# Two more places for weight chunks, an earlier (1,0) vector, and the first down weights asked for by GpSimd

## The reference, cut to what matters

```python
cs = silu(c)
for i in range(2):
    mod = cs @ w_mod[i] + b_mod[i]                    # 1024 x 6144: 24 MB a layer
    sh_m, sc_m, g_m, sh_f, sc_f, g_f = split(mod, 6)
    h = modulate(rmsnorm(x, norm_mix[i]), sh_m, sc_m)
    y = hybrid_ab(h, ...) if i == 0 else multiscale_pool(h, w_pool, pool_scale)
    x = x + g_m * y
    h = modulate(rmsnorm(x, norm_ffn[i]), sh_f, sc_f)
    x = x + g_f * hier_moe(h, ...)
return rmsnorm(x, norm_out)

# hybrid_ab: proj = h @ w_in (q, kv, index queries qi, index key, u, v); attention over
#   the 64 keys that the index scores pick; spatial gating of u by v; concat @ w_o
# multiscale_pool: means over trailing windows of 2, 4, 8, 16 tokens, minus h, per-group
#   256x256 matmul (w_pool), times pool_scale
# hier_moe: 4 groups x 8 experts, softmax over groups, best group, best 2 experts in it;
#   out = sum over experts of (silu(t @ w_gate) * (t @ w_up) * gate) @ w_down
```

## Time and profile before

| what | value |
|---|---|
| time, median of 3 | 732.12 us (731.3 to 732.17) |
| the profiled execution | 731.96 us |
| its span | 729.5 us |
| TensorE busy | 641.2 us (88%) |
| VectorE busy | 372.6 us (51%) |
| ScalarE busy | 174.0 us (24%) |
| read from memory | 268.16 MB, mean 370 GB/s with writes |

### The profile page before, as it was taken

One profiled execution on the slowest core, in us unless ns is written; L12 is line 12 of the kernel. 1 busy time (PEld: TensorE's weight loads), 2 busy tenths in 40 slices (PEclk: granted clock), 3 DMA queues, 4 the chain that ended last, 5 costly groups with the idle time before them and its releaser, 6 DMA issues.

```text
span 729.5 us, 11410 instructions
## 1 busy us (share of the span) xinstructions
PE 641.2 (88%) x4226; PEld 386.8 (53%) x4226; DVE 372.6 (51%) x902; ACT 174.0 (24%) x370; POOL 24.9 (3%) x54
## 2 busy tenths in 40 slices
PE   2699998999998889988899888999898899888994
PEld 1487565466654545445554445775445455455542
DVE  1268868967644533443334477664344334433345
ACT  2113441033411211122112240342113111221113
POOL 5100400000000000000000000000000000000000
PEclk9999999999999999999999999799999999999998
DMA  8999535997699999999999999887999999999991
GB/s 335 351 398 398 174 116 192 410 360 281 256 421 421 421 421 423 422 421 423 422 422 422 417 399 409 338 339 306 423 422 420 420 422 422 422 421 423 422 392 58
DMA packets 49677, 269.61 MB, mean 370 GB/s; under 512 B 3796, under 2 KB 5908, under 8 KB 25072
## 3 DMA queue, kind: packets, MB, share of 16 engines
q1 hardware_dynamic: 48864, 268.22, 90.6%
q0 software_dynamic: 784, 1.00, 0.7%
HBM read 268.16 MB, written 1.05 MB: 369 GB/s over the span
## 4 chain that ended last, share of the span: by engine, by line
PE 48%; DMA 38%; SPq 5%; DVE 5%; issue 2%; ACT 1%; POOL 0%; DVEq 0%; POOLq 0%; ACTq 0%
DMA ring<-in_w_up 35%; PE bank L875 9%; PE bank L854 8%; PE bank L889 5%; PE bank L592 4%; PE bank L739 4%; DMA early_w<-in_w_in 3%; PE bank L804 2%; PE bank L522 2%; PE bank L664 2%; PE bank L674 2%; PE bank L759 1%; PE bank L842 1%; SPq L346 1%; PE bank L627 1%
## 5 line engine op out<-in xcount | busy, mean ns | idle before, releaser
L854 PE MATMUL bank<-ring,arena 128*64 128x256 f32 x1024 | 117.3, 382 | 28.9 <-DMA ring<-in_w_up 28.8
L842 PE MATMUL bank<-ring,arena 128*64 128x256 f32 x1024 | 117.6, 382 | 12.8 <-DMA ring<-in_w_gate 12.8
L1139 ACT CAST xn_parts<-arena 128x512 fp32r<-128x512 f32 x64 | 39.6, 619 | 305.6 <-DVE arena L1591 305.6
L854 PEld LDWEIGHTS bank<-ring,arena 128*64 128x64 f32 x1024 | 71.1, 137 | 74.3 <-DMA ring<-in_w_up 41.2
L875 PE MATMUL bank<-dn_w,hT 128*64 128x512 f32 x480 | 109.5, 598 | 0.7 <-DMA dn_w<-in_w_down 0.7
L842 PEld LDWEIGHTS bank<-ring,arena 128*64 128x64 f32 x1024 | 81.1, 137 | 41.9 <-issue 16.8
L1566 DVE SCALAR_TENSOR_TENSOR hT<-hT,bank 128x256 f32<-128x256 f32 x32 | 19.8, 619 | 118.1 <-PE bank L854 118.1
L889 PE MATMUL bank<-xn_parts,sel 128*128 128x512 f32 x256 | 67.1, 406 | 0.0
L875 PEld LDWEIGHTS bank<-dn_w,hT 128*64 128x64 f32 x480 | 32.0, 136 | 62.4 <-issue 61.0
L1591 DVE SCALAR_TENSOR_TENSOR arena<-bank,hT,gates 128x512 f32<-128x512 f32 x64 | 48.0, 749 | 23.5 <-PE bank L875 23.5
L889 PEld LDWEIGHTS bank<-xn_parts,sel 128*128 128x128 f32 x256 | 45.8, 188 | 20.9 <-issue 12.4
(11 more groups left out here) (282 smaller groups left out, 676.1 us busy)
## 6 DMA issues: line engine op xcount, KB each, us to landing
ring<-in_w_gate SPq DMA_DIRECT2D x32, 2048.0 KB, 13.7
ring<-in_w_up SPq DMA_DIRECT2D x32, 2048.0 KB, 18.2
dn_w<-in_w_down SPq DMA_DIRECT2D x30, 2048.0 KB, 10.3
ring<-in_w_mod SPq DMA_DIRECT2D x23, 2048.0 KB, 16.5
ring<-in_w_in SPq DMA_DIRECT2D x2, 2048.0 KB, 21.1
ring<-in_w_down SPq DMA_DIRECT2D x2, 2048.0 KB, 14.6
early_w<-in_w_in SPq DMA_DIRECT2D x1, 2048.0 KB, 21.0
dn_w<-in_w_in SPq DMA_DIRECT2D x1, 2048.0 KB, 17.2
```

The costliest lines, as they stand in the source:

```text
L842: ins = pe.matmul(bank[2][h * WIN:(h + 1) * WIN, 0:FE], xw[:, b, h, k, :], w[:, h, 0, k, :], start=(k == 0), stop=(k == KT - 1))
L854: ins = pe.matmul(bank[3][h * WIN:(h + 1) * WIN, 0:FE], xw[:, b, h, k, :], w[:, h, 1, k, :], start=(k == 0), stop=(k == KT - 1))
L1139: act.copy(xn_parts[:, 0, b, at], y_s[:, b, at]).then_inc(e["y_hi"], 1)
```

## The change

Line numbers in the diff's words are those of the kernel before; the rows of the changed program below have its own.

- **Places.** Two halves of `arena` (free once the attention's values are done) become places for n1a and n1b, the halves of (1,1). The halves of (1,0) move ahead: n0a is loaded right after m2b, n0b after v. q, v, u and the halves of (0,4) and (0,3) come one or two places later, or in other slots. The expert pairs of layer 0 use slots (1,2) and (0,3) instead of (0,2) and (1,3).
- **(1,0) on PE.** Its first half stands between the third and the fourth group of index scores, its second half after the first two transposes of the attention weights. Both leave the routing stage.
- **Waits of SP.** The first expert pair waits for DVE's use of m3b, the second for m5a and the second output chunk; before they waited for PE's use of n0b and n1b.
- **First down weights of layer 0.** GpSimd (POOL) asks for them after DVE's use of m5b; before, SP did so ahead of its loop.
- **Constant rows.** The row of `norm_mix` is spread ahead of kv and no longer after the scores. `pool_scale` is spread in the middle stage ahead of the pooling matmuls, and DVE reads it from PSUM. The halves of `norm_out` are spread after the first pooling matmul group and after (1,4).
- Smaller: (0,2) is reduced into banks 2 and 7; two semaphores of the experts' loop become one.

```diff
-        front = [..., (("in", "kv"), ATT), (("in", "qi"), EARLY_W),
-                 (m2a, 0), (m2b, 1), (("in", "q"), ATT), (("in", "v"), 3), (("in", "u"), 2), (m4a, 0), (m4b, 1),
-                 (("out", 0), EARLY_W), (("out", 1), 3), (m3a, 0), (m3b, 2), (m5b, ATT), (m5a, 1), (n0a, 0), (n0b, 2), (n1a, 1), (n1b, 3)]
+                 (m2a, 0), (m2b, 1), (n0a, 2), (("in", "q"), ATT), (("in", "v"), 3), (n0b, 0), (("in", "u"), 1),
+                 (("out", 0), EARLY_W), (m4a, 2), (("out", 1), 3), (m4b, 0), (m3a, 1), (m3b, 2), (m5b, ATT), (n1a, ARENA_A),
+                 (m5a, 0), (n1b, ARENA_B)]
-        PAIRS = (((0, 2), (1, 3)), ((0, 1), (2, 3)))
+        PAIRS = (((1, 2), (0, 3)), ((0, 1), (2, 3)))
...
             for n in range(FIRST):                                          # SP
                 slot_freed(sp, n)
-                if plan[n] == m5b:
+                if slot_of(n) in (ARENA_A, ARENA_B) or plan[n] == m5b:
                     sp.wait_ge(S["p_turned"], 6)
                     sp.wait_ge(S["bT_ready"], 1)
+                    sp.wait_ge(S["pv_done"], 4)
                 chunk(n)
...
-                sp.wait_ge(S["chunk_done"], chunk_no[n0b if l == 0 else ("mod", 21)] + 1)
+                if l == 0:
+                    sp.wait_ge(S["dve_used"], by_dve.index(m3b) + 1)
+                else:
+                    sp.wait_ge(S["chunk_done"], chunk_no["mod", 21] + 1)
                 gate_load(l, 0, 0)
                 up_load(l, 0, 0)
-                sp.wait_ge(S["chunk_done"], chunk_no[n1b if l == 0 else ("mod", 23)] + 1)
+                if l == 0:
+                    sp.wait_ge(S["dve_used"], by_dve.index(m5a) + 1)
+                    sp.wait_ge(S["chunk_done"], chunk_no["out", 1] + 1)
+                else:
+                    sp.wait_ge(S["chunk_done"], chunk_no["mod", 23] + 1)
                 gate_load(l, 1, 2)
                 up_load(l, 1, 2)
-                if l == 0:
-                    sp.wait_ge(S["dve_used"], by_dve.index(m5b) + 1)
-                else:
+                if l == 1:
                     sp.wait_ge(S["mix_done"], 10)
-                down(l, 0)
+                    down(l, 0)
...
             power(1)                                                        # POOL
+            pool.wait_ge(S["dve_used"], by_dve.index(m5b) + 1)
+            pool.dma_start(dn_w[:, :].rearrange("p o t d -> p o (t d)"),
+                           w_down[0][0:2].rearrange("o (p t) d -> p o (t d)", t=FT)).then_inc(S["dn_first"], 16)
...
-            head_units(range(6), qiT, kiT, (3, 4, 6), S["score_done"], S["score_relu"])   # PE
+            units = qiT, kiT, (3, 4, 6), S["score_done"], S["score_relu"]
+            head_units(range(3), *units)
+            vector((1, 0), (0,))
+            head_units(range(3, 6), *units)
...
+            pe.wait_ge(S["wsT_copied"], 1)
             reduce((0, 2))
             pe.wait_ge(S["kvnT_ready"], 1)
-            pe.wait_ge(S["wsT_copied"], 1)
...
             turn_p(0)
             turn_p(1)
+            vector((1, 0), (1,))
...
                 if l == 0:                                                  # route
-                    turn_raw(l, (0,)), vector((1, 0), (0,)), turn_raw(l, (1,)), vector((1, 0), (1,))
+                    turn_raw(l)
                 else:
-                    vector((1, 3), (1,)), vector((1, 4), (0,)), turn_raw(l), vector((1, 4), (1,))
+                    vector((1, 3), (1,))
+                    pe.wait_ge(S["row_kept"], 1)
+                    vector((1, 4), (0,)), turn_raw(l), vector((1, 4), (1,))
+                    pe.wait_ge(S["col_kept"], columns.index((1, 3)) - 1)
+                    norm_out_row(1, bank[0])
...
                 if l == 0:
                     vector((1, 1), (0,))
-                    for row, b in ((SCALE_ROW, 2), (OUT_ROW, 4)):
-                        for half in range(2):
-                            pe.matmul(bank[b + half][:, :], ident[:, row:row + 1].to_broadcast([P, P]), rows[:, half * HALF:(half + 1) * HALF],
-                                      start=True, stop=True).then_inc(S["row_done"], 1)
...
+            def norm_out_row(half, to):
+                pe.matmul(to[:, :], ident[:, OUT_ROW:OUT_ROW + 1].to_broadcast([P, P]), rows[:, half * HALF:(half + 1) * HALF],
+                          start=True, stop=True).then_inc(S["row_done"], 1)
...
+            for half in range(2):                                           # middle stage, PE
+                ins = pe.matmul(bank[2 + half][:, :], ident[:, SCALE_ROW:SCALE_ROW + 1].to_broadcast([P, P]), rows[:, half * HALF:(half + 1) * HALF],
+                                start=True, stop=True)
+            ins.then_inc(S["row_done"], 1)
             pe.wait_ge(S["wpool_in"], 16)
             for g in range(4):
+                if g == 1:
+                    pe.wait_ge(S["mod_kept"], 6)
+                    norm_out_row(0, bank[1])
...
-            done(tt(gates[:, 2, :], gates[:, 2, :], gates[:, 3, :], ALU.mult))   # DVE
+            dve.wait_ge(S["row_done"], 1)
+            for half in range(2):
+                at = slice(half * HALF, (half + 1) * HALF)
+                ins = tt(gates[:, 2, at], gates[:, 2, at], bank[2 + half][:, :], ALU.mult)
+            done(ins)
```

More of the change, by code:

```diff
@@ L246, in free_banks @@
             past = turns[:turns.index(vec)]
-            gates_past = [v for v in past if v in GATE]
+            gates_past = [v for v in past if v in GATE and v != (0, 2)]
             if gates_past:
@@ L536, in reduce @@
                     for half in range(2):
-                        pe.matmul(bank[half][:, :], ones[:], vec_sum[vec][:, half * HALF:(half + 1) * HALF], start=True, stop=True
+                        pe.matmul(bank[banks_of(vec)[half]][:, :], ones[:], vec_sum[vec][:, half * HALF:(half + 1) * HALF], start=True, stop=True
                                   ).then_inc(S["gate_done"], 1)
@@ L605, in _ @@
             vector((0, 1), (1,))
+            for q in range(4):
+                ins = pe.matmul(bank[7][32 * q:32 * q + 32, 0:KT * 32].rearrange("p (k i) -> p k i", k=KT),
+                                ident[:, GAIN_ROW:GAIN_ROW + 1].to_broadcast([P, 32]), by_quadrant(rows[:, :], q, True),
+                                start=True, stop=True)
+            ins.then_inc(S["gain_row"], 1)
             w = arrived(("in", "kv"))
@@ L639, in _ @@
             ins.then_inc(S["ws_turned"], 1)
-            for q in range(4):
-                ins = pe.matmul(bank[2][32 * q:32 * q + 32, 0:KT * 32].rearrange("p (k i) -> p k i", k=KT),
-                                ident[:, GAIN_ROW:GAIN_ROW + 1].to_broadcast([P, 32]), by_quadrant(rows[:, :], q, True),
-                                start=True, stop=True)
-            ins.then_inc(S["gain_row"], 1)
+            pe.wait_ge(S["wsT_copied"], 1)
             reduce((0, 2))
             pe.wait_ge(S["kvnT_ready"], 1)
-            pe.wait_ge(S["wsT_copied"], 1)
-            by_channel(("in", "q"), (5, 7), S["q_done"])
-            pe.wait_ge(S["gain_ready"], 1)
+            by_channel(("in", "q"), (5, 7), S["q_done"], (S["mod_kept"], 2))
             pe.wait_ge(S["wkv_ready"], 1)
@@ L955, in keep_gate @@
                     act.wait_ge(S["gate_done"], 2 * gated.index(vec) + half + 1)
[L956 removed]
+                    act.copy(gates[:, GATE[vec], half * HALF:(half + 1) * HALF], bank[banks_of(vec)[half]][:, :]).then_inc(S["mod_kept"], 1)
             def keep_column(vec):
@@ L1078, in _, with keep_row @@
             keep_heads(1)
+            def keep_row(half, source):
+                act.wait_ge(S["row_done"], 2 + half)
+                act.copy(gates[:, 0, half * HALF:(half + 1) * HALF], source[:, :]).then_inc(S["row_kept"], 1)
             def route(l):
@@ L1097, in route @@
                 if l == 0:
-                    for n, b in ((3, 2), (0, 4)):
-                        for half in range(2):
-                            act.wait_ge(S["row_done"], b - 1 + half)
-                            act.copy(gates[:, n, half * HALF:(half + 1) * HALF], bank[b + half][:, :]).then_inc(S["row_kept"], 1)
-                    keep_column((1, 0)), keep_column((1, 1))
+                    keep_column((1, 1))
                 else:
```

67 lines of the change are left out of this document (39 added, 28 removed).

## The result

The changed kernel took 738.53 us, the median of five runs (735.84 to 739.52), beside 732.12 us for the kernel before (731.3 to 733.45, five runs). The ratio is 1.006, 95% interval [1.0034, 1.0087]: slower by some 0.6%. The profiled execution took 738.75 us and its span is 736.5 us, 7.0 more than before.

A forecast was written before the change was run, and what follows sets the result against it. Bound taken: the experts' loop loads at 421 to 423 GB/s, plus when each loop gets into its stride. Terms -2.5 + 2.2 - 1.3 + 0.5 - 1.4 = -2.5 us from 731.96, plus 0.16, gave 729.6 us; range 726.6 to 732.9.

The forecast's parts named there:

- the first down weights: Layer 0's first `down`: POOL's load shares evenly with SP's loads and lands late, a stall of +2.2 us, bounds 0 and 4.1.
- counting starts past 171: Sign of being wrong: layer 0's first counting matmul, forecast near 169.5 us, starts later than 171.
- the third: Third sign of being wrong: the logits of layer 0 take 6 us or more.
- The 7.8 us row: Profile row cited for even sharing: a 256 KB POOL load beside a full SP queue took 7.8 us; its bytes need 0.6.
- served last: Upper bound at the first `down`: POOL's load comes last, three loads of 15 us from 189.5, landed at 205.5, +4.1 us.
- Attention stage, +2.65: Halves of (1,0) put into the attention stage delay it: +2.05 us before q, +0.6 for the second; bounds 0.5 and 4.2.
- Routing stage shorter, net -2.5: Layer 0 routing without (1,0)'s halves and the constant rows: counting starts at 169.55, not 172.12; -2.5 us net for the early part.
- TensorE's clock in layer 0, +0.5: Clock may fall sooner: 0 to +3.0 us at layer 0's logits, +1.4 more at the gather; taken as +0.5.
- The rival of this name: Slower by layer 0's clock: low clock covers logits (+3.0) and gather start (+1.4), layer 1 gains nothing; 734.9 us, chance 0.13.
- Less queueing, -1.3: Layer 0's switch to waiting for loads: third load behind the freeing takes 18.93 us instead of 20.23, -1.3 us.
- Layer 1, -1.4: Layer 1 routing: a `norm_out` row in PE's idle time keeps the clock up for the logits, -1.4 us, bounds -3.0 and 0.2.
- Early chunks, 0: Loading n0a and n0b in the hole at 73 to 128 us moves 9.9 us of loads early; worth 0, up to +0.5.

The follow-up runs named there:

- e2: Changed kernel with SyncE's loop held until GpSimd's first down weights have landed: 737.1 us, ratio 1.0056 to the kernel before.
- e3: Kernel before with one part of the change alone, GpSimd asking for layer 0's first down weights: 736.58 us, ratio 1.0057.
- e9: Changed kernel with the edits of e5 and e6, GpSimd still asking for the first down weights: 733.18 us, ratio 1.0005.
- e1: Changed kernel with SyncE again asking for the first down weights ahead of its loop, not GpSimd: 730.52 us, ratio 0.9971.
- e8: e1 with SyncE's first pass asking gate, down, up instead of down, gate, up: 730.75 us, ratio 0.9963.
- e5: e1 with (0,2) reduced into its old banks, ahead of the wait for ScalarE's copy: 728.66 us, ratio 0.9939.
- e6: e5 with two unread constant-row matmuls in TensorE's pause before layer 0's counting: 727.22 us, ratio 0.9912.
- e4: Kernel before with one unread constant-row matmul behind (1,4) in layer 1's routing stage: 731.94 us, ratio 0.999.
- the first group: First of three groups of experiment kernels, each group run on one chip beside the kernel before; that kernel's median there was 733.29 us.

## Why the prediction was wrong

The time missed the forecast by 8.9 us (738.53 for 729.6). By the profile 5.6 of them are the first down weights (5.4 + 2.4 where 2.2 stood) and 4.3 the attention and routing stages (+1.8 where -2.5 stood); the forecast's own +0.5 for the clock, and 0.3 in layer 1, come off again, which leaves 9.1. The recorded sign "counting starts past 171" came (171.24), and so did a pause of the DMA engines in the loop of layer 0; the logits of layer 0, at 4.23 us, stayed below the 6 of the third.

- **Failed step: the first down weights.** Taken at +2.2 with a bound of 4.1; it cost 5.4 us of wait and 2.4 of low clock, and 4 to 7 us in the three pairs that differ in it. The even share was right, as the two loads that end within 1.2 us of each other show: the up load, asked for first, took 14.1 us, and served in order of issue it would have ended one load, 4.97 us, ahead of the other. With the rule of the Trainium skill that the prediction cited ("DMA: Bandwidth & Descriptors", Queues, rings and completion order) these 14.1 us agree. Right was also the time at which PE needs the weights (10.0 us after the issue, 10.1 forecast). The load's fixed part was wrong: 2.1 us ahead of the data and 0.2 behind, against 4.4 together when it runs alone (e2). Then 9.94 + 4.4 = 14.3 us, as measured in e3 and e9 (14.2, 14.3; 15.2 in the changed kernel), not 12.3. The earlier trace rows had it: 18.93 us for three loads of 4.97 leave 4.0 around them, and the forecast used that very row for another term. The 7.8 us row had it too. It was read for the share alone, while the trace of the kernel before shows, from the same queue and 1.2 us earlier,

```profile
kvg<-in_kv_norm POOLq DMA_DIRECT2D x1, 0.5 KB, 5.9
```

so most of those 7.8 us did not belong to the bytes. The bound for "served last" had the same fault, and its sum is not of one piece: 189.5 + 15 is 204.5, to which 1.0 is added up to landing, where the middle took 0.2.
- **Missed: what follows a wait.** No price stood beside the wait for the low clock behind it. `down` ran in 6.04 us for 3.60 (5.35 in e3, 6.55 in e9); where the wait moved to the gate load, so did the low clock (e2). The earlier trace rows showed the pattern, a pause and then half clock, and the forecast applied it to the routing stages alone.
- **Attention stage, +2.65: measured +4.2.** The wait for ScalarE's copy was seen, the low clock on the reduction behind it (+1.67) not. That low clock is no fixed price (absent in e1 and e8, where the reduction takes 1.98 us; there again in e2); the wait is, and e5 takes it away: q at 62.30.
- **Routing stage shorter, net -2.5: measured +1.8 at the first `gate_half`.** The half vectors left the path as said. The late start took 1.6 of it (4.2 for 2.65), another 0.1 to 0.2 went at the logits (4.23 for 4.01), and 2.7 went behind the start of the counting, whose clock fell behind the 1.95 us pause that the constant rows had filled. "Constant rows gone" was booked as pure gain; with two rows put back that have no other use the low clock is gone (e6).
- **TensorE's clock in layer 0, +0.5.** The rival of this name ended on the right side, but for the most part not by its own mechanism: the logits kept their clock (4.23 us). Its +1.4 at the start of the gather came, one step earlier and as 2.7; the other falls, before q and at the first `down`, it did not have.
- **Less queueing, -1.3: right** (18.95 measured). e8 has 18.70.
- **Layer 1, -1.4: not shown.** The profile had -1.7, the run of that row alone no difference (e4), and the same code took 4.08 to 6.89 us in other profiles. The number was near by luck. The Trainium skill ("TensorE: Matmul & The Clock Gate", What's actually happening) has the monitor run free of the program and meet it at another phase from run to run. The 4.08 to 6.89 us in the same code agree with it. The forecast set three runs 0.9 us apart against it; the 30 runs of the kernel before in the first group span 729.7 to 736.7 us.
- **Early chunks, 0: right.** The loads came earlier and their users did not, so the DMA engines stood idle from 176 to 192 us.

## What to carry to other kernels

Price a transfer by its data at the share it will have plus the fixed part that an undisturbed one shows, and compare that with the moment of need. Here a request from a second queue, 0.1 us behind another, overtook nothing, and both took over 14 us; ahead of the others in one queue it came in time. To every new wait of TensorE add the slow matmuls that may stand behind it, and before taking work out of a pause ask whether it kept the clock up. A term that hangs on the clock's phase is tested by pairs of runs, not read off one profile.

## What the runs showed that was not expected

- A 2 MB load alone took 9.4 us from issue to landing, from GpSimd's queue; 4.97 of it is data. With two others beside it 14.2 to 15.2. A load of 0.5 KB from that queue, beside a busy SyncE queue, took 5.9.
- Matmuls that nobody reads made the kernel's counting and gather start 2.7 us closer together (5.67 for 8.35 us), in each profile that has them, and delayed the counting itself by 0.2 to 0.5.
- Where the clock falls differs between profiles of the same code: the logits of layer 0 took 5.89 us in e1_sp_down and 3.74 in e8_gate_first, whose programs part only behind them.
